# GQA row maxima in 64 rows of TensorE's array, two groups of 512 keys in its two halves, and a layout of the score operands that fits it

## What is computed

```python
def gqa_attend(q, k, v):
    s = jnp.einsum('bqhgd,bkhd->bhgqk', q, k).astype(jnp.float32) * (GQA_HEAD_DIM ** -0.5)
    p = jax.nn.softmax(s, axis=-1).astype(v.dtype)
    return jnp.einsum('bhgqk,bkhd->bqhgd', p, v)
...
    k_all = jnp.concatenate([kc, k], axis=1)
    v_all = jnp.concatenate([vc, v], axis=1)
    o = sweep_query_blocks(lambda qb: gqa_attend(qb, k_all, v_all), q).reshape(B, S, GQA_WIDTH)
    ...
        oc = gqa_attend(qc, kc, vc).reshape(B, L, GQA_WIDTH)
```

## Time and profile before

| | |
|---|---|
| median of 3 executions | 3566.96 us (3566.53 to 3567.2) |
| the profiled execution's own time | 3564.46 us |
| its span | 3562.7 us |
| PE busy over the span | 3386.1 us (95%), 15156 matmuls |
| DVE / ACT / POOL busy | 2187.2 (61%) / 1790.9 (50%) / 1534.3 us (43%) |
| granted TensorE clock over the span | 0.988 of full speed |

### The profile page before, as it was taken

One profiled execution on the slowest core, in us unless ns is written; L12 is line 12 of the kernel. 1 busy time (PEld: TensorE's weight loads), 2 busy tenths in 40 slices (PEclk: granted clock), 3 DMA queues, 4 the chain that ended last, 5 costly groups with the idle time before them and its releaser, 6 DMA issues.

```text
span 3562.7 us, 48300 instructions
## 1 busy us (share of the span) xinstructions
PE 3386.1 (95%) x15156; PEld 2681.3 (75%) x15156; DVE 2187.2 (61%) x2655; ACT 1790.9 (50%) x3060; POOL 1534.3 (43%) x977
## 2 busy tenths in 40 slices
PE   7999999999999999899999999899988999999999
PEld 5777887778888888687876777678665667777777
DVE  6674878477575766537346666666558875555551
ACT  3343878232010101334258888861465657877870
POOL 3303444544444444510156666656210026666652
PEclk9999999999999999999999999999999999999999
DMA  2134231311212121122433443412254334232311
GB/s 100 49 117 126 62 90 55 146 38 58 89 55 87 46 96 40 52 101 107 147 85 75 94 91 71 103 65 89 98 207 148 124 108 123 54 82 53 77 42 71
DMA packets 196087, 313.54 MB, mean 88 GB/s; under 512 B 100928, under 2 KB 111680, under 8 KB 195968
## 3 DMA queue, kind: packets, MB, share of 16 engines
q1 hardware_dynamic: 195968, 312.01, 29.8%
HBM read 234.02 MB, written 77.92 MB: 88 GB/s over the span
## 4 chain that ended last, share of the span: by engine, by line
PE 68%; DVE 12%; issue 7%; ACT 6%; POOL 3%; DMA 2%; SPq 2%; DVEq 0%; ACTq 0%; POOLq 0%
PE PBX L281 10%; PE PBX L283 10%; PE PBX L282 10%; PE PMX L281 5%; PE PMX L282 5%; PE PMX L283 5%; PE PMX L1966 4%; PE PD L2007 2%; PE PD L2008 2%; PE PD L2009 2%; PE PD L868 2%; DVE gqa_m L2098 1%; PE PBX L1991 1%; PE PBX L1990 1%; PE PBX L1992 1%
## 5 line engine op out<-in xcount | busy, mean ns | idle before, releaser
L216 POOL TENSOR_TENSOR w_hi<-w_stage,zero 128x1024 fp32r<-128x1024 f32 (+2 forms) x123 | 226.9, 1845 | 1251.8 <-PE PBX L283 759.5
L2076 POOL TENSOR_TENSOR gqa_pl<-gqa_pf,gqa_ph 128x512 fp32r<-128x512 f32 (+1 forms) x288 | 371.7, 1309 | 184.9 <-ACT gqa_ph L2049 184.0
L2076 POOL TENSOR_TENSOR mla_pl<-mla_pf,mla_ph 128x512 fp32r<-128x512 f32 x256 | 351.8, 1383 | 205.8 <-ACT mla_ph L2049 201.6
L2098 DVE TENSOR_REDUCE gqa_m<-PMX 128x1 f32<-128x1280 f32 (+1 forms) x158 | 200.9, 1272 | 168.7 <-PE PMX L1966 168.0
L218 POOL TENSOR_TENSOR w_lo<-w_stage,w_hi 128x1024 fp32r<-128x1024 f32 (+2 forms) x123 | 300.1, 2440 | 9.7
L1691 ACT ACTIVATE conv_in<-PBX 128x512 f32<-128x512 f32 x66 | 39.5, 600 | 480.7 <-PE PBX L283 476.7
L2098 DVE TENSOR_REDUCE mla_m<-PMX 128x1 f32<-128x1280 f32 x126 | 187.4, 1487 | 87.6 <-PE PMX L1966 87.2
L2044 ACT ACTIVATE mla_pf<-PBX 128x512 f32<-128x512 f32 x320 | 189.8, 593 | 97.2 <-PE PBX L1992 87.3
L2044 ACT ACTIVATE gqa_pf<-PBX 128x512 f32<-128x512 f32 (+1 forms) x352 | 201.8, 573 | 52.9 <-PE PBX L1995 48.6
L2049 ACT ACTIVATE gqa_ph<-gqa_pf 128x512 fp32r<-128x512 f32 (+1 forms) x352 | 215.6, 613 | 13.8
L281 PE MATMUL PBX<-ffn_hi,w_hi 128*128 128x512 f32 x528 | 206.8, 392 | 3.8 <-DVE ffn_lo L665 3.8
(11 more groups left out here) (415 smaller groups left out, 9978.4 us busy)
## 6 DMA issues: line engine op xcount, KB each, us to landing
mod_w<-in_w_mod SPq DMA_DIRECT2D x48, 512.0 KB, 3.5
w_stage<-in_w_up SPq DMA_DIRECT2D x44, 512.0 KB, 3.5
w_stage<-in_w_go SPq DMA_DIRECT2D x24, 512.0 KB, 3.7
gqa_k<-kh_d SPq DMA_DIRECT2D x32, 320.0 KB, 4.9
gqa_q<-qh_d SPq DMA_DIRECT2D x32, 320.0 KB, 7.6
w_stage<-in_w_down SPq DMA_DIRECT2D x24, 384.0 KB, 3.0
qh_d<-heads_qh SPq DMA_DIRECT2D x32, 256.0 KB, 2.0
ql_d<-heads_ql SPq DMA_DIRECT2D x32, 256.0 KB, 2.3
```

Of the source, the lines that this page charges most:

```text
L216: pool.tensor_tensor(w_hi[s][:, 0:st.cols], w_stage[s][:, 0:st.cols], z, ALU.add).then_inc(w_hi_done, 1)
L2076: eng.tensor_tensor(self.PL[k % 4][:, 0:n], self.PF[k % 4][:, 0:n], self.PH[k % 4][:, 0:n].bitcast(F32), ALU.subtract).then_inc(self.lo_dv ...
L2098: dve.tensor_reduce(self.M[g % 2][:, t:t + 1], MX[:, 0:w], AX.X, ALU.max, negate=True)\
```

## The change

For GQA all four operands now have 128 rows. K1 is ones in rows 0 to 63 and the high halves of the keys in rows 64 to 127; Q1 has the low halves of the queries in rows 64 to 127 and, in rows 0 to 63, zeros except row 0, which takes minus the maximum. The second score matmul has 128 rows instead of 65. The maxima use 64 rows, high halves only: the groups of 512 keys alternate between rows 0 to 63 (Q0 by K0) and rows 64 to 127 (Q0 by K1, which is why the high halves of the keys moved there), so that in a full group the three matmuls take half 0, half 1, half 0; a single takes half 0. `const_dve` writes 64 rows of ones in place of one, and has a fourth memset of zeros. ACT's copy of the maxima reads and writes row 0 instead of row 64. MLA's numbers come out as before.

```diff
-            kr, qr = ((97, 96), (97, 96)) if layout == "mla" else ((P, 65), (P, 65))
+            kr, qr = ((97, 96), (97, 96)) if layout == "mla" else ((P, P), (P, P))
...
-                self.row = 96 if self.mla else 64
+                self.row = 96 if self.mla else 0
...
-                self.const_n = 3 + (32 if self.mla else 0)
+                self.const_n = 35 if self.mla else 4
...
-                    parts = [(K[0][0:64, :], kh), (K[0][64:128, :], kl), (K[1][0:64, :], kh)]
+                    parts = [(K[0][0:64, :], kh), (K[0][64:128, :], kl), (K[1][64:128, :], kh)]
...
-                parts = [(Q[0][0:r, :], qh), (Q[1][0:r, :], ql)] + ([] if self.mla else [(Q[0][64:128, :], qh)])
+                parts = [(Q[0][0:r, :], qh), (Q[1][0:r, :] if self.mla else Q[1][64:128, :], ql)] + ([] if self.mla else [(Q[0][64:128, :], qh)])
...
-                dve.memset(self.K[q][0 if self.mla else 1][self.row:self.row + 1, :].bitcast(F32), 1.0)\
-                   .then_inc(self.const[q], 1)
+                ones_rows = self.K[q][0][96:97, :] if self.mla else self.K[q][1][0:64, :]
+                dve.memset(ones_rows.bitcast(F32), 1.0).then_inc(self.const[q], 1)
+                if not self.mla:
+                    dve.memset(self.Q[q][1][0:64, :].bitcast(F32), 0.0).then_inc(self.const[q], 1)
...
-                mr = self.dim if self.mla else P
...
-                        mm = pe.matmul(MX[:, s - lo_:e - lo_], self.Q[q][0][0:mr, o:o + P], self.K[q][0][0:mr, s:e],
+                        half = 0 if self.mla else (s - lo_) // C % 2
+                        rows = slice(64 * half, 64 * half + self.dim)
+                        mm = pe.matmul(MX[:, s - lo_:e - lo_], self.Q[q][0][rows, o:o + P], self.K[q][half][rows, s:e],
                                        start=True, stop=True)
```

## The result

Twenty executions of each kernel: the changed one takes 3575.19 us, the one before 3564.98; the ratio is 1.0032, 95% interval 1.0025 to 1.0038, some 11 us slower. The forecast was 18.5 us slower. The profiled execution of the changed kernel took 3567.46 us (span 3565.7), the shortest of its twenty; its granted clock over the span is 0.993, that of the one before 0.988, so the two whole spans (3.0 us apart) can't be compared. So I compare the stage itself: from the first group of maxima to the last it takes 550.9 us (1804.9 to 2355.7) where it took 540.5 (1805.4 to 2345.9), 10.4 more.

The account below looks back on a forecast made before the run. PE was taken to bound the GQA stage, with waits. 16 heads x (1.28 - 0.19) = 17.4 us plus 1.1 for the memset, some 18.5, gave 3585.5 us, 0.5% slower; range 3549 to 3607.

Parts of the forecast that it names:

- full groups: Three-matmul maxima groups: -0.23 us plus two switches at steps 12, 18, 0, 6; plus one at 16, 4.
- singles: Lone 256-key maxima matmuls at steps 8 and 10: each pays two switches and saves nothing.
- load wait no longer there: PE's query-load wait at step 12, 3.0 us over 6 heads, vanishes: -0.19 us a head.
- layout, 65 to 128 rows: Second score matmul going from 65 to 128 rows: same spacing, so nothing.
- The switch: Each passage between 128-row and 64-row matmuls drains the array: 0.19 us, between 0 and 0.27.
- The overlap: Second matmul of a full group runs beside the first in the other half: saves 0.23 us.
- The cover at 14 and 2: Full groups at these steps stand ahead of longer waits, which swallow costs up to 0.3 to 0.4 us.
- The memset: DVE's added memsets delay the second reduction of the second chunk at the stage's start: 1.1 us later, once.
- The sign that I had named: In the trace, PE's 1.92 us wait at the stage's start would be longer by about 1.1 us.
- free switches: Rival: the array changes to 64 rows without emptying, x = 0, kernel faster at 3551 us; chance 27%.
- no overlap: Rival: the halves run one behind the other, 0.23 us not saved, 3608 us; chance 14%.
- break-even: Rival: a switch costs 0.06 to 0.13 us, an exposed weight load only, 3560 to 3572 us; chance 14%.

Follow-up runs that it names:

- the layout alone: Changed kernel with the maxima back in 128 rows, everything else as changed: ratio 0.9995 to the kernel before, 34.19 us a head.
- early loads: Transfers reordered to keys, queries, values, the values on their own semaphore; on the kernel before: ratio 0.9978, 33.90 us a head.
- the probe: Kernel before plus 74 matmuls of ones ahead of the stage, switching row counts and halves: 0.43 us at each 64/128 change, 0.23 a pair in different halves.
- one half: Changed kernel with all maxima in rows 0 to 63, none in the other half: ratio 1.0083 to the kernel before.
- the variant with the late multiplications: Reordered loads and DVE's two chunk-end multiplications two steps later: ratio 1.0014 on the kernel before, 1.0046 on the changed kernel, both against before.

## Why the prediction was right, and where not

The direction and the mechanism were right: half of the array costs more at its borders than the overlap gives. The size was too large, 18.5 us forecast, some 11 measured. With the load out of the way, heads separate the terms:

| term, us a head | forecast | measured | from |
|---|---|---|---|
| full groups | +0.52 | +0.51 | 34.25 - 33.74 |
| singles | +0.76 | +0.76 | 35.01 - 34.25 |
| load wait no longer there | -0.19 | -0.43 | 33.90 - 34.33 |
| layout, 65 to 128 rows | 0 | -0.16 | 33.74 - 33.90 |
| sum | +1.09 | +0.68 | 35.01 - 34.33 |

The load's term is confirmed by a second pair, the layout alone without and with early loads (34.19 and 33.74), the layout's by the pair without early loads (34.33 and 34.19).

**The switch.** Taken at 0.19 between 0 and 0.27; measured 0.19 to 0.20 in the kernel and 0.20 in the probe. The exposed weight load of 0.11 was right as read from a group behind idle time; the emptying is 0.09, not the 0.16 by which the modelled end of a row overhangs. That half of the 0.16 came so close was luck: no row stood behind the half.

**The overlap.** Taken at the whole 0.23, and it is.

**Which groups are on the path.** The sum of the full groups is right by luck. The step that failed is that the group at 6 pays in full and those at 16 and 4 keep a saving. The 0.51 us are three groups, at 12, 18 and 0, at 0.17 each; of the group at 6 the wait for the diagonal at step 8 takes back 0.13 (it stands in the earlier trace rows, and the prediction doesn't count it as cover), and the rest cancels the saving at 4; the saving at 16 goes into the value matmul behind it, which waits for DVE's low part. The forecast's 0.52 are four groups at 0.15 less two savings of 0.04. The cover at 14 and 2 was right, and so was the group at 12: from the broadcast ahead of it to the second score matmul it takes 1.09 us after the change (2008.08 to 2009.17) and 0.92 with early loads before it.

**The load.** The step "the load wait of 3.0 us (0.19 a head) vanishes" undersized the term: with the load early, a head lost 0.43. The wait stood in all heads and not in six, and with it came an exposed weight load; the wait's own row shows neither. This is the largest part of the error. It also carried the one expectation that went against me, the singles: they saved 0.76, and the load took back more than half.

**The rest.** "So nothing" for 65 against 128 rows was wrong by 0.16 us a head, in the change's favour. The memset was right: from the first diagonal on DVE to the end of the reduction behind the memsets it takes 6.06 us (1811.20 to 1817.26) where it took 5.01 (1811.97 to 1816.98), 1.05 more. The sign that I had named did not show, though. In the layout alone the wait there is 2.99 us, 1.07 longer; in the changed kernel it is 1.44, shorter than the 1.92 of before:

```profile
1816.20 1.44 PE L1969 MATMUL PMX<-gqa_k,gqa_q 128*128 128x512 f32 x3 [2.99 <-DVE gqa_m L2101]
```

```profile
1817.31 0.61 PE L1969 MATMUL PMX<-gqa_k,gqa_q 64*128 64x512 f32 x3 [1.44 <-DVE gqa_m L2101]
```

```profile
1808.00:1814.00 6.00, 5.58 (x15) 3.72 (x15) 5.60 (x7) 0.00 (x0) 0.00 (x0) 0.50 1.18 214
```

PE itself came late: behind a wait of 1.24 us for the first reduction (1.00 before, where the clock stayed at 1.00), the changed kernel ran from 1807.6 to 1814.4 at the 1.2 GHz level. It cost nothing, since DVE ended last. The two groups ahead of the diagonal are 0.23 us shorter, so the start of the stage is 0.8 longer in all.

Together: 16 x 0.68 + 0.8 = 11.7 us, against the 11 of the ratio. The stage in the traces grew by 10.4, since the last head counted there is 1.5 us shorter after the change (34.91 against 36.43): before, it has an idle stretch of 1.8 us at 2314.6 and 3.4 us at the 1.2 GHz level behind it.

The rivals fell as follows: free switches by the probe and the weight loads, no overlap by the probe and by one half, break-even because x is twice what it needs.

## What to carry to other kernels

Using half the array pays only if the stretch in that mode is long enough: here a pair of 512 columns gives 0.23 us and the way in and out takes 0.39, so a visit of one pair loses, and a lone 256-column matmul in 64 rows costs four times as much (0.50 us for 0.12). By these numbers two pairs a visit would just pay, an estimate that no run here tried. Before counting such a price, look at what stands around the group: behind a wait the way in is free, and ahead of a longer wait all of it is. And when a change seems to do nothing, look for a transfer that waits at the same place; taking that one away first made every other term readable. A wait that a variant makes longer can also bring the clock down behind it, so read the granted clock before putting a difference down to the edit.

## What the runs showed that I had not expected

A 65-row matmul among those of 128 slows its surroundings slightly. With it, the first two value matmuls behind it follow each other after 0.240 us (mean of 262 spacings in the kernel with early loads), and with 128 rows throughout after 0.234 (265 spacings); the head is 0.16 us shorter. The layout also moves operands to other rows, and no run separates that from the row count.

Matmuls in different halves start together, although each has its own weights: in the probe both loads lie ahead, and in the kernel, behind a switch, the two loads run side by side too (three loads in 0.29 us at 2011.34, where one takes 0.18).

DVE's instructions with both operands in SBUF stretch when they meet POOL. In the variant with the late multiplications, the diagonal and the gate's product take up to 1.49 and 1.55 us; in the kernel before the same diagonal takes 0.69 to 1.07, the product 0.42.

```profile
1997.74 1.55 DVE L2136 TENSOR_TENSOR MIX<-gqa_t,gqa_gate 64x256 f32 x1
1999.22 1.48 DVE L2112 TENSOR_REDUCE gqa_m<-PMX 128x1 f32<-128x1280 f32 x1
2000.73 1.49 DVE L2120 TENSOR_TENSOR gqa_d<-ident_f,gqa_m 128x512 fp32r<-128x512 f32 x1
...
1997.72 5.65 POOL L2090 TENSOR_TENSOR gqa_pl<-gqa_pf,gqa_ph 128x512 fp32r<-128x512 f32 x4 [1.47 <-ACT gqa_ph L2063]
```

The multiplication before the gate's, which has one operand in PSUM, keeps its time in both kernels (0.41 to 0.69 us). The Trainium skill (SBUF — State Buffer, SBUF: two separate sides) says that a DVE instruction with two SBUF inputs and a GpSimd instruction that reads SBUF exclude each other for the whole of one; these rows agree.
